# Attention units: the causal block added by TensorE, identities scaled by ScalarE, three convolution taps in a unit

## The reference, cut to what matters

```python
q = partial_rope(q, positions); k = partial_rope(k, positions)
def one_block(args):                       # 128 queries, 4 heads, 2 components c
    sc = jnp.einsum("bhcqd,bhckd->bhcqk", q_blk, k) * scale        # d = 64, scale = 1/8
    sc = jnp.where(mask, sc, -jnp.inf)                             # causal
    p = jax.nn.softmax(sc, axis=-1)
    a = p[:, :, 0] - lam * p[:, :, 1]
    return jnp.einsum("bhqk,bhkv->bhqv", a, v)
...
c = u[..., :CV_WIDTH] * jax.nn.sigmoid(u[..., CV_WIDTH:])
c = causal_dwconv(c, cv_dw_w) + cv_dw_b                            # 31 taps, 512 channels
```

## Time and profile before

| | us |
|---|---|
| median of 3 runs | 3458.84 |
| lowest and highest of them | 3457.24, 3459.06 |
| the profiled execution, its time | 3455.18 |
| its span, from the first instruction to the last | 3453.0 |
| busy in the span: PE | 3319.9 |
| busy in the span: DVE | 2295.0 |
| busy in the span: POOL | 1838.0 |
| busy in the span: ACT | 774.1 |

### The profile page before, as it was taken

One profiled execution on the slowest core, in us unless ns is written; L12 is line 12 of the kernel. 1 busy time (PEld: TensorE's weight loads), 2 busy tenths in 40 slices (PEclk: granted clock), 3 DMA queues, 4 the chain that ended last, 5 costly groups with the idle time before them and its releaser, 6 DMA issues.

```text
span 3453.0 us, 40759 instructions
## 1 busy us (share of the span) xinstructions
PE 3319.9 (96%) x15978; PEld 2733.3 (79%) x15978; DVE 2295.0 (66%) x3397; ACT 774.1 (22%) x1201; POOL 1838.0 (53%) x994
## 2 busy tenths in 40 slices
PE   7989899999999999999999999999999999999998
PEld 5777678887876787888788888888888888888887
DVE  6975279963326256777563888799974437777784
ACT  2132322211126222222211111145530111111110
POOL 4536367766542454100466666643346666767675
PEclk9989999999999999999999999999999999999999
DMA  3212122222220122000232443445453336555552
GB/s 134 74 56 92 49 86 93 97 98 91 98 74 31 62 85 67 19 13 13 92 104 98 139 142 138 137 165 204 181 201 122 117 121 195 189 195 190 194 185 96
DMA packets 164270, 391.70 MB, mean 113 GB/s; under 512 B 10736, under 2 KB 69104, under 8 KB 162032
## 3 DMA queue, kind: packets, MB, share of 16 engines
q1 hardware_dynamic: 73408, 262.70, 22.6%
q10 hardware_dynamic: 90672, 126.39, 10.7%
HBM read 326.14 MB, written 62.91 MB: 113 GB/s over the span
## 4 chain that ended last, share of the span: by engine, by line
PE 71%; DVE 24%; issue 2%; ACT 2%; POOL 0%; DMA 0%; DVEq 0%; ACTq 0%; POOLq 0%
PE banks L1389 19%; PE banks L1390 19%; PE banks L1391 19%; DVE sb_gated L1295 6%; DVE sb_sq L2034 3%; DVE sb_onehot L1292 2%; PE banks L706 2%; PE banks L369 1%; PE banks L717 1%; DVE sb_tmp L2044 1%; DVE banks L1911 1%; PE banks L714 1%; PE banks L386 1%; DVE sb_tmp L1335 1%; DVE sb_sq L2032 1%
## 5 line engine op out<-in xcount | busy, mean ns | idle before, releaser
L1377 POOL TENSOR_TENSOR sb_wL<-sb_raw,sb_wH 128x1024 fp32r<-128x1024 f32 x495 | 1209.4, 2443 | 1583.3 <-PE banks L1391 1516.1
L1389 PE MATMUL banks<-sb_hH,sb_wH 128*128 128x512 f32 x2040 | 822.4, 403 | 8.4 <-issue 2.4
L1390 PE MATMUL banks<-sb_hL,sb_wH 128*128 128x512 f32 x2040 | 801.1, 393 | 0.0
L1391 PE MATMUL banks<-sb_hH,sb_wL 128*128 128x512 f32 x2040 | 800.8, 393 | 0.0
L1372 POOL TENSOR_SCALAR sb_wH<-sb_raw 128x1024 fp32r<-128x1024 f32 x495 | 644.5, 1302 | 14.9 <-DMA sb_raw<-in_weights 14.9
L1389 PEld LDWEIGHTS banks<-sb_hH,sb_wH 128*128 128x128 f32 x2040 | 387.5, 190 | 95.1 <-issue 14.3
L1391 PEld LDWEIGHTS banks<-sb_hH,sb_wL 128*128 128x128 f32 x2040 | 386.8, 190 | 82.6
L1390 PEld LDWEIGHTS banks<-sb_hL,sb_wH 128*128 128x128 f32 x2040 | 387.9, 190 | 78.3 <-issue 3.6
L1389 PE MATMUL banks<-sb_pzH,sb_wH 128*128 128x512 f32 x1024 | 400.1, 391 | 8.4 <-DVE sb_pzL L1339 6.3
L1390 PE MATMUL banks<-sb_pzL,sb_wH 128*128 128x512 f32 x1024 | 398.6, 389 | 0.0
L1391 PE MATMUL banks<-sb_pzH,sb_wL 128*128 128x512 f32 x1024 | 398.6, 389 | 0.0
(11 more groups left out here) (420 smaller groups left out, 4797.9 us busy)
## 6 DMA issues: line engine op xcount, KB each, us to landing
sb_raw<-in_weights SPq DMA_DIRECT2D x495, 512.0 KB, 3.2
gates<-sb_stage ACTq DMA_DIRECT2D x16, 2048.0 KB, 7.7
acts<-sb_sq ACTq DMA_DIRECT2D x96, 256.0 KB, 2.0
sb_Gt<-gates ACTq DMA_DIRECT2D x24, 1024.0 KB, 7.1
sb_Ga<-acts ACTq DMA_DIRECT2D x24, 1024.0 KB, 10.0
sb_Gt<-gates ACTq DMA_DIRECT2D x4, 2048.0 KB, 10.1
sb_xT<-in_xT SPq DMA_DIRECT2D x4, 512.0 KB, 10.5
acts<-sb_xT ACTq DMA_DIRECT2D x1, 2048.0 KB, 7.8
```

Of the source, the lines that this page charges most:

```text
L1377: nc.gpsimd.tensor_tensor(wL[:, t % LOS, :], raw[:, t % RAWS, :], wH[:, t % HIS, :].bitcast(F32), ALU.subtract).then_inc(sems("weights_lo" ...
L1389: pe.matmul(out, hi, H, start=start, stop=False)
L1390: pe.matmul(out, hi, L, start=False, stop=False)
L1391: return pe.matmul(out, lo, H, start=False, stop=stop)
```

## The change

The last block's mask is now added by PE. After each score matmul a second matmul with the identity as its weights and `causal` as its moving data adds into the same bank. For this the sign is turned: ACT multiplies the queries by -0.125 when it copies them (the keys by 1), `causal` is 0 or +1e30, DVE takes a minimum instead of a maximum, and its result is the exponential's bias directly, with scale -1. The two scaled identities are made by ACT, the second one from an identity that holds minus lambda (`lam_ident`, made once by DVE). DVE reports the reciprocals by a new semaphore, `recip`, between its first tap of the unit and the other two.

The convolution runs 76 taps ahead of the first meeting instead of 92, and three in each unit instead of two. Lane 0 is finished ahead of the meeting, its last 38 taps without lane 1 between them; all 48 taps in the units are lane 1. Their sums stay in PSUM: bank 7 is copied to bank 1 once after the first unit's minimum, and bank 1 is moved to `cacc` between groups 1 and 3 and at the end. Bank 1 is kept free by putting all `mk` tiles into bank 0; before they alternated between banks 0 and 1.

```diff
--- before.py
+++ after.py
@@ -86,8 +86,9 @@
     _up = 0 <= _t - TILE["up"] < 44
+    _keys = 0 <= _t - TILE["mk"] < 8
     _rows = 0 <= _t - TILE["in_v"] < 4 or 0 <= _t - TILE["mv"] < 8 or 0 <= _t - TILE["sb_v"] < 8
-    BANK.append(None if _down or _rows else (0, 1, 6, 3)[_t % 4] if _u else (0, 1, 5, 6)[(_t - TILE["up"]) % 4] if _up else (7, 0)[(_t - TILE["z"]) % 2] if _z else 7 if _gate else (0, 1, 7)[_t % 3] if _conv else _t % 2)
+    BANK.append(None if _down or _rows else (0, 1, 6, 3)[_t % 4] if _u else (0, 1, 5, 6)[(_t - TILE["up"]) % 4] if _up else (7, 0)[(_t - TILE["z"]) % 2] if _z else 7 if _gate else 0 if _keys else (0, 1, 7)[_t % 3] if _conv else _t % 2)
     BEFORE_IN_BANK.append(0 if _down or _rows else BANK[:_t].count(BANK[_t]))
@@ -108,7 +109,7 @@
     put("swap", swap)
-    put("causal", np.where(r[None, :] <= r[:, None], 0.0, NEG))
+    put("causal", np.where(r[None, :] <= r[:, None], 0.0, -NEG))
     put("low", r[:, None] > r[None, :])
@@ -541,6 +542,7 @@
 
+        lam_ident = dg[:, 1, S - P:S]
         parts = [(2, slice(offs[2], 1280), slice(0, 1280 - offs[2])), (1, slice(offs[1], offs[2]), slice(0, qw[1])),
@@ -1490,9 +1492,11 @@
                         r = slice(64 * c, 64 * c + 64)
-                        nc.tensor.matmul(ps[2 + 2 * (u % 2) + c][:, 0:P * (i + 1)],
-                                                  B["qkT"][r, h, i * P:(i + 1) * P],
-                                                  B["qkT"][r, 4 + h, 0:P * (i + 1)], start=True, stop=True).then_inc(sems("scores"), 1)
+                        z = ps[2 + 2 * (u % 2) + c]
+                        nc.tensor.matmul(z[:, 0:P * (i + 1)], B["qkT"][r, h, i * P:(i + 1) * P],
+                                         B["qkT"][r, 4 + h, 0:P * (i + 1)], start=True, stop=True)
+                        nc.tensor.matmul(z[:, i * P:(i + 1) * P], ident, C("causal"), start=False, stop=True,
+                                         skip_group_check=True).then_inc(sems("scores"), 1)
 
@@ -1695,7 +1699,10 @@
                     hi_part(E, B["mH"][:, k, :], NMEM)
-                copy_tiles("in_qk", 8, lambda b: B["qkT"][:, b, :])
+                for b in range(8):
+                    t = TILE["in_qk"] + b
+                    tile_ready(E, t)
+                    empties(act.activation(B["qkT"][:, b, :], bank(t), ACT.Copy, scale=-0.125 if b < 4 else 1.0), t)
                 tile_ready(E, TILE["in_v"] + 3)
@@ -1708,13 +1715,17 @@
                         act.activation(B["p"][:, u % 2, c, 0:w], ps[2 + 2 * (u % 2) + c][:, 0:w], ACT.Exp,
-                                                bias=ss[:, u % 2, 2 + c:3 + c], scale=0.125,
+                                                bias=ss[:, u % 2, c:c + 1], scale=-1.0,
                                                 accum_out=ss[:, u % 2, 4 + c:5 + c]).then_inc(sems("probs"), 1)
...
                         probabilities(u + 1)
+                    E.wait("recip")
+                    E.at("att_turned", u - 1)
+                    act.activation(B["att"][:, u % 2, 0:P], ident, ACT.Copy, scale=ss[:, u % 2, 6:7])
+                    act.activation(B["att"][:, u % 2, P:2 * P], lam_ident, ACT.Copy, scale=ss[:, u % 2, 7:8]).then_inc(sems("att"), 1)
                     if u % 2:
@@ -1883,14 +1894,14 @@
                 order = [(0, j) for j in range(10)]
-                for j in range(52):
+                for j in range(14):
                     order += [(1, j), (0, j + 10)]
-                order += [(1, j) for j in range(52, 62)]
-                place = [ps[5][:, :], ps[7][:, :]]
+                order += [(0, j) for j in range(24, 62)] + [(1, j) for j in range(14, 62)]
+                place = [ps[5][:, :], ps[7][:, :], ps[1][:, :]]
 
...
 
-                    chain(v.tensor_copy(B["cacc"][:, m, :], place[lane]))
+                    chain(v.tensor_copy(B["cacc"][:, m, :], place[2 if m % 2 else lane]))
 
@@ -1903,7 +1914,7 @@
                         x = B["cpad"][:, m, k:k + S]
-                        sum_ = place[lane] if n < SPLIT else B["cacc"][:, m, :]
+                        sum_ = place[lane if n < SPLIT else 2]
                         if k == 0:
@@ -1911,7 +1922,7 @@
 
-                SPLIT = 4 * TAPS - 2 * len(units)
+                SPLIT = 4 * TAPS - 3 * len(units)
                 gate(0)
@@ -1936,11 +1947,10 @@
                     v.tensor_tensor(q, q, tmp[:, b % 2, :], ALU.add).then_inc(sems("roped"), 1)
-                    taps(44 + 5 * b, 49 + 5 * b)
-                taps(84, SPLIT)
+                    taps(44 + 4 * b, 48 + 4 * b)
                 E.at("tap", SPLIT)
                 move(0, 2)
-                move(1, 3)
+                v.tensor_scalar(lam_ident, ident, sc[:, 6:7], None, ALU.mult)
                 E.meet()
@@ -1948,23 +1958,21 @@
                     E.wait("scores", 2)
-                    last = z[:, :, i * P:(i + 1) * P]
-                    chain(v.tensor_tensor(last, last, C("causal").unsqueeze(1).to_broadcast([P, 2, P]), ALU.add))
-                    chain(v.tensor_reduce(ss[:, o, 0:2], z, AX, ALU.max))
-                    v.tensor_scalar(ss[:, o, 2:4], ss[:, o, 0:2], -0.125, None, ALU.mult).then_inc(sems("row_max"), 2)
+                    v.tensor_reduce(ss[:, o, 0:2], z, AX, ALU.min).then_inc(sems("row_max"), 2)
 
                 maxima(0)
+                chain(v.tensor_copy(place[2], place[1]))
                 for u, (h, i) in enumerate(units):
...
                         maxima(u + 1)
-                    taps(SPLIT + 2 * u, SPLIT + 2 * u + 2)
+                    taps(SPLIT + 3 * u, SPLIT + 3 * u + 1)
                     o = u % 2
                     E.wait("probs", 2)
-                    chain(v.reciprocal(ss[:, o, 6:8], ss[:, o, 4:6]))
-                    chain(v.tensor_scalar(ss[:, o, 8:9], ss[:, o, 7:8], sc[:, 6:7], None, ALU.mult))
-                    E.at("att_turned", u - 1)
-                    v.tensor_scalar(B["att"][:, o, 0:P], ident, ss[:, o, 6:7], None, ALU.mult)
-                    v.tensor_scalar(B["att"][:, o, P:2 * P], ident, ss[:, o, 8:9], None, ALU.mult).then_inc(sems("att"), 1)
+                    E.at("att", u - 1)
+                    v.reciprocal(ss[:, o, 6:8], ss[:, o, 4:6]).then_inc(sems("recip"), 1)
+                    taps(SPLIT + 3 * u + 1, SPLIT + 3 * u + 3)
+                E.at("tap", 4 * TAPS)
+                move(1, 3)
                 E.meet()
...
                 for k in range(4):

```

## The result

Over 20 runs each the changed kernel took 3461.03 us and the kernel before 3455.11 us (medians); the ratio is 1.0017, interval 1.0010 to 1.0023. That is 5.9 us more, 3.5 to 8 by the interval, and inside the bound of 0.2%, though the upper end of the interval lies just outside it. With 20 runs the kernel before stands 3.7 us lower than with the three that I had; I compare differences. One run of the changed kernel took 4801 us and is left out of the ratio. The profiled execution has a span of 3458.6 us, 5.6 more than before.

The account below looks back on a forecast made before the run. DVE narrowly bounds the units, then PE. First turn 165.4 plus 78.0 us work and 1.2 waiting ends at 244.6, 1.1 later; the profiled 3455.2 becomes 3456.3, plus 3.7 for the median gives 3459.9 us, range 3450 to 3466.

Parts of the forecast that it names:

- The bound: In the units: DVE bounds them, not by much; after the change PE does, 21.7 us a group against 20.4.
- Ahead of the meeting: Before the units' first scores: DVE ends near 151.6, ACT is late next, the meeting moves to 156.15, gain 1.6 us.
- DVE in a unit: DVE's work per unit falls from 4.70 to 3.1 us, with over 1.5 us to spare.
- ACT: ACT in the units: identities at 0.3 us each, busy 9.7 us a group; 1.2 us of PE waiting at the end.
- PE's scores: Masks between the components' scores make them serial, adding 0.85 + 0.213 w, 1.38 us in a mean unit.
- The sum: Over the units PE's last turn ends at 244.6, 1.1 us later than now; net +1.1 us.
- one spell at the low clock as today's groups have it: Before the first turn: PE loses 8% of 20.4 us, 1.6 us, to a lowered clock.
- (1): Rival, units: the clock falls in each group, 2.0 us a group, +8.4, 3467 us; chance 0.13.
- (2): Rival, units: the score pair still overlaps, form costs nothing, group some 18.2 us, -11.4, 3447.5 us; chance 0.13.
- (3): Rival, units: components serial but no cost of the form, 0.40 us less a unit, -5, 3454 us; chance 0.17.
- (4): Rival, units: DVE stays the bound, at best today's pace, 3457 us; chance 0.05.

Follow-up runs that it names:

- e11: The changed kernel unaltered, run and profiled again on another chip; ratio to the kernel before 1.0010 (1.0001 to 1.0019).
- e6: e2 with 92 taps ahead of the first meeting and two in a unit, as before the change; ratio to the kernel before 0.9952.
- e2: The changed kernel with the causal mask added by DVE again, one instruction over both components; ratio to the kernel before 0.9958.
- e1: The changed kernel with both score matmuls of a unit first, then both mask matmuls; 3449.23 us, ratio to the kernel before 0.9983.
- e4: The changed kernel with each mask matmul over its component's own 64 rows, omitting half the causal block; ratio to the kernel before 0.9954.
- e9: The changed kernel with unread matmuls before the first meeting and the first half key tile between scores of units 0 and 1; ratio to the kernel before 1.0000.
- e5: e2 with the two scaled identities made by DVE again instead of ACT; ratio to the kernel before 0.9951.

## Why the prediction was right, point by point

**The bound.** Right: DVE bound the units by a little, and PE took over. A group has 21.64 us; I had 21.7.

**The number.** I forecast 3459.9 and the median is 3461.03, but that nearness is luck: I had put the kernel before 3.7 us too high, from three runs. As a difference it is +1.1 against +5.9 (3.5 to 8), or +3.2 in e11. The mechanism came as forecast; one term of the sum did not.

**Ahead of the meeting.** DVE's end near 151.6: measured 152.7, with the stage 0.5 us later in that execution. ACT late next: right. Gain 1.6: measured 1.2 in the profile, 1.7 without that shift. No whole time shows it; e6, which tried, is too coarse.

**DVE in a unit.** 3.1 us: measured 12.89/4 = 3.2. The taps in a bank measured 0.75 us each, where rows 5 had given me 0.79.

**ACT.** The record of a scaled identity is 0.40 us, not 0.3, but the next one starts after 0.29 (e2's timeline), and ACT's busy time is 9.49 us a group where I had 9.7. PE's wait fell to 0.7 us, against 1.2 in my sum.

**PE's scores.** The step on which the forecast stood. 0.85 + 0.213 w added: measured 1.70 for width 4 and 1.07 for width 1, where I had 1.70 and 1.06, from start of the scores to start of the keys. e1 and e4 show the mechanism: the bare masks cost 1.4 us a group (17.94 against 16.53 in e2), what the place of the masks adds is another 3.7. The drain that the Trainium skill names in "TensorEngine Tiling (Array Packing)", Key Properties, agrees with the gaps of about 0.1 us on each side of the narrow matmuls. It is the smaller part: of the 3.7 us a group, 2.1 are the lost overlap (0.213 us for each of ten blocks).

**The sum.** +1.1 us forecast, +5.9 measured (3.5 to 8). The term that was mis-sized is "one spell at the low clock as today's groups have it", 1.6 us. The spell at the start lasts 10.2 us, and all of it now falls on PE's work: from the first scores to the first turn it is 11.65 us, where my 7.5 us of work leave 4.1 lost (e9, without the spell, takes 7.7 in all). It was as long before the change (156.1 to 166.4), but there it lay over the two waits of the start, as the windows of the kernel before show:

```profile
156.00:160.00 4.00, 1.66 (x8) 0.96 (x8) 2.65 (x7) 0.15 (x1) 1.57 (x2) 0.52 0.37 131
160.00:164.00 4.00, 1.69 (x5) 0.62 (x5) 3.34 (x10) 3.00 (x9) 0.00 (x0) 0.50 0.00 0
164.00:168.00 4.00, 4.00 (x20) 3.23 (x20) 3.65 (x9) 0.84 (x4) 0.00 (x0) 0.70 0.00 0
```

They would have told me; I took the groups' 0.92. That is 2.5 of the 3.0 us by which the first turn was late; the first scores, 0.4 us after my 156.35, are the rest. From the first turn to the last turn's end the trace has 78.8 us and my sum 79.2. Another 2 us in the profile lie behind the units, where the changed kernel's profile had 6 us more of low clock; e11 had 10 less than the kernel before, so this is not shown to be the change's.

**The rivals.** (1), a fall of the clock in each group, didn't come; the clock was 1.00 there. A spell at the low clock did cost PE's time, but at the start. (2), components side by side, is what e1 and e4 make of it: 17.94 and 17.23 us a group against my 18.2. (3), serial without a cost of the form, would be 0.40 us less a unit, 20.1 us a group; with 21.64 measured it is out. (4) is out too.

**What each part is worth**, in the units' block: the changes other than mask and identities (sums in a bank, the scaling folded into the queries, the product with lambda gone) take it from 88.3 to 75.0 us (e5); no run separates them, and e6 shows only that the third tap in a unit costs nothing. The identities on ACT take it to 72.0 (e2). The mask on PE adds 6.8 in pairs (e1), and 21.2 as the change has it; the spells at the low clock, 6.8 us in e2 and e5 and 10.2 in e1 and the changed kernel, are in these numbers. The mask as placed eats what all the other parts gain. One part of the 13.3 us stands in the kernel before's trace. The scaling of the maximum (L1954, two columns) takes 0.17 us, but four of the 16 take 1.7 to 2.3, each of them ending with a tensor operation of POOL that had begun before it:

```profile
190.93 1.85 DVE L1954 TENSOR_SCALAR sb_ss<-sb_ss 128x2 f32<-128x2 f32 x1
...
190.39 2.37 POOL L1377 TENSOR_TENSOR sb_wL<-sb_raw,sb_wH 128x1024 fp32r<-128x1024 f32 x1 [5.01 <-PE banks L1391]
```

That is 7.1 us of DVE's time over the four, and the change has no such instruction; how much of it reached the units' length no run shows.

## What to carry to other kernels

Before a small matmul is given to TensorE, look at what it would stand between: two matmuls over 64 rows each, on different rows, run side by side, and one over all 128 rows between them costs their overlap and two changes of form besides its own time. Here a unit paid 1.28 us over e2 for two masks that take 0.45 by themselves. Keep narrow matmuls together and put the wide ones behind them. And when an engine is relieved, count the full work of the next one from a clean stretch at full clock first: PE had 16.2 of 20.4 us, which left room for the bare masks and not for the place they were given.

## What the runs showed of the hardware

- The two passes of an fp32 matmul over rows 0 to 63 and those over rows 64 to 127 start together (170.858 and 170.865 us in the kernel before) although one component's passes are both issued first; even a mask between them keeps this, if it is narrow too (e4).
- PE at work without a gap is not enough for a high clock. The changed kernel's PE is busy without a break from 156.7 us on, and the clock fell at 159.3 and stayed at half for 10.2 us; in e11 for 13.7. With 12 dense matmuls among the first scores and the waits filled it ran at 1.00 (e9, one profile).
- A copy of 128 columns with a pointer as its scale takes ACT 0.40 us from SBUF, 0.29 from start to start, against 0.28 for a plain one from a bank.
- A VectorE instruction on two columns can take 2.3 us instead of 0.17 while POOL works on a tile of 128 x 1024 (L1954, 4 times of 16).
- The same 3200 us of program varied by 11 us from one profile to the next, twice the difference between the two kernels.
